# GpSimd runs through its eight S5 tables without waiting, in the fourth, for the first splits of the down projection

## What is computed

```python
h = rms_norm(x, norm_ffn1_g)
gate, up = jnp.split(h @ w_up, 2, axis=-1)
x = x + 0.5 * ((silu(gate) * up) @ w_down)          # w_down: 2816 x 1024

abar_re = exp(dt*a_re) * cos(dt*a_im)               # S5: one complex pole per state
abar_im = exp(dt*a_re) * sin(dt*a_im)
# its powers, times B and C, feed the scan over the sequence in the mixer
```

## Time and profile before

| | |
|---|---|
| median of three runs | 2174.9 us (2174.46 to 2175.28) |
| time of the profiled execution | 2173.43 us |
| its span in the profile | 2171.2 us |
| PE busy | 2136.7 us (98%) |
| DVE busy | 1701.8 us (78%) |
| POOL busy | 656.8 us (30%) |

### The profile page before, as it was taken

How to read it: one execution, slowest core, us unless ns; L and a number is a source line. 1 busy time by engine, 2 the same in 40 slices (tenths; PEclk the granted TensorE clock), 3 DMA queues, 4 the chain that set the end, 5 groups by cost and what they waited for, 6 DMA issues and landing times.

```text
span 2171.2 us, 31658 instructions
## 1 busy us (share of the span) xinstructions
PE 2136.7 (98%) x10191; PEld 1767.2 (81%) x10191; DVE 1701.8 (78%) x2163; ACT 946.5 (44%) x1560; POOL 656.8 (30%) x749
## 2 busy tenths in 40 slices
PE   7999999999999999999999999999999999999998
PEld 6788888888888888888888788887888888888886
DVE  5877878879975999999998659767687768665557
ACT  6455555544455122222224224135455555544444
POOL 2886667979930000000000430500024442000000
PEclk9999999999999999999999999999999999999999
DMA  5335885488783344544445642985156764337764
GB/s 172 80 120 163 273 281 193 150 287 293 252 278 120 99 145 143 162 130 150 154 124 166 215 135 78 322 307 197 61 184 203 232 213 160 102 114 264 232 194 174
DMA packets 316194, 397.43 MB, mean 183 GB/s; under 512 B 28625, under 2 KB 201265, under 8 KB 315984
## 3 DMA queue, kind: packets, MB, share of 16 engines
q1 hardware_dynamic: 293264, 315.71, 45.4%
q0 software_dynamic: 21104, 76.24, 10.4%
q10 hardware_dynamic: 1744, 4.46, 0.5%
HBM read 266.81 MB, written 129.52 MB: 183 GB/s over the span
## 4 chain that ended last, share of the span: by engine, by line
PE 92%; DVE 5%; ACT 1%; DMA 1%; issue 1%; SPq 0%; DVEq 0%; ACTq 0%
PE PU L1503 11%; PE PU L1504 11%; PE PU L1505 11%; PE PU L1443 9%; PE PU L1445 9%; PE PU L1444 9%; PE PD L1378 4%; PE PD L1380 4%; PE PD L1379 4%; PE PU L1378 3%; PE PU L1380 3%; PE PU L1379 3%; PE PD L1579 1%; PE PD L1580 1%; PE PD L1581 1%; PE PU L1474 1%
## 5 line engine op out<-in xcount | busy, mean ns | idle before, releaser
L1443 PE MATMUL PU<-Hhi,Whi 128*128 128x512 f32 x896 | 352.2, 393 | 0.8 <-issue 0.7
L1445 PE MATMUL PU<-Hhi,Wlo 128*128 128x512 f32 x896 | 348.9, 389 | 0.0
L1444 PE MATMUL PU<-Hlo,Whi 128*128 128x512 f32 x896 | 348.7, 389 | 0.0
L2609 DVE SCALAR_TENSOR_TENSOR XT<-XT,wq 128x1024 f32<-128x1024 f32 x240 | 311.8, 1299 | 8.2
L1443 PEld LDWEIGHTS PU<-Hhi,Whi 128*128 128x128 f32 x896 | 168.2, 188 | 38.7 <-issue 3.5
L1445 PEld LDWEIGHTS PU<-Hhi,Wlo 128*128 128x128 f32 x896 | 168.2, 188 | 35.4
L1444 PEld LDWEIGHTS PU<-Hlo,Whi 128*128 128x128 f32 x896 | 168.3, 188 | 34.8 <-issue 0.7
L1503 PE MATMUL PU<-Hhi,Dhi 128*128 128x512 f32 x480 | 186.8, 389 | 0.5 <-ACT s1b L1857 0.5
L1505 PE MATMUL PU<-Hhi,Dlo 128*128 128x512 f32 x480 | 186.7, 389 | 0.0
L1504 PE MATMUL PU<-Hlo,Dhi 128*128 128x512 f32 x480 | 186.7, 389 | 0.0
L1378 PE MATMUL PD<-Dhi,Ahi 128*128 128x512 f32 x416 | 162.5, 391 | 2.8 <-DVE Alo L2183 2.8
(11 more groups left out here) (414 smaller groups left out, 5072.0 us busy)
## 6 DMA issues: line engine op xcount, KB each, us to landing
TAB<-in_w_ffn_down POOLq DMA_DIRECT2D x44, 512.0 KB, 5.0
d_sb<-TAB POOLq DMA_DIRECT2D x44, 512.0 KB, 4.0
Wraw<-in_w_ffn_up SPq DMA_DIRECT2D x80, 256.0 KB, 4.6
XT<-in_w_ffn_up SPq DMA_DIRECT2D x80, 256.0 KB, 4.4
d_sa<-XT SPq DMA_DIRECT2D x80, 256.0 KB, 2.3
Wraw<-in_w_in SPq DMA_DIRECT2D x32, 512.0 KB, 5.2
d_act<-G SPq DMA_DIRECT2D x48, 256.0 KB, 2.1
WRd<-d_sb SPq DMA_DIRECT2D x44, 256.0 KB, 4.2
```

Source lines behind the costliest of these rows:

```text
L1443: mm(o_, Whi[s][:, side, k, :], Hhi[:, k, hs[h]], start=k == 0, stop=False)
L1444: mm(o_, Whi[s][:, side, k, :], Hlo[:, k, hs[h]], start=False, stop=False)
L1445: last = mm(o_, Wlo[s][:, side, k, :], Hhi[:, k, hs[h]], start=False, stop=k == KT - 1)
L2609: stt(CVb, z_, w_, CVb, ALU.mult, ALU.add).then_inc(m["conv"], 1)
```

## The change

The wait of GpSimd in table 3 is taken out. No instruction is added, removed or put in another place on any engine.

```diff
             pool.dma_start(d_tab[q, :, T_CAR:T_COS], TAB[:, T_CAR:T_COS]).then_inc(ca_saved, 16)
 
-            if q == 3:
-                pool.wait_ge(rd_lo, RING + 4)
             step(g.tensor_copy(M8q, M8[:, r4]))
             pool.wait_ge(pool_ld[0], 16 * TAKES + q * 16 + 16)
```

## The result

The changed kernel takes **2179.13 us** (median of 20 runs, 2176.16 to 2184.33); the kernel before, in 20 runs beside it, 2174.51 us. The ratio is 1.002, with a 95% interval of 1.0014 to 1.0026: 3.0 to 5.7 us slower, where +3.0 us and 2177.9 us had been forecast. The interval excludes no change, and by the bound of 0.2% the difference is right at the edge of what counts as the same.

The account below looks back on a forecast made before the run. PE was taken to bound the kernel; +3.0 (early waits) - 0.8 (old wait gone) + 0.8 (new late wait) = +3.0 us on 2173.4 gave 2176.4, and the median 1.5 above it 2177.9 us; range 2174.6 to 2180.6.

Parts of the forecast that it names:

- What bounds the kernel: Whole kernel: PE busy 2136.7 of 2171.2 us sets the end; its down projection had one split wait, 0.8 us.
- The turns: DVE splits beside GpSimd tensor operations: one such DVE operation gets through for each GpSimd operation.
- The narrow part: Table 3's smaller operations beside the first splits: turns add 1.4 us by step 3; PE waits 0 to 0.5, taken 0.2.
- The first wide part: GpSimd's 512- and 576-wide operations, 469.8 to 489.7 us: PE has lost 3.0 us by step 11, pieces at step 3 included.
- The rival with one turn fewer: Step 6's first split is caught too: PE 4.8 us late, 2179.7 us; chance 0.26, shared with the late wait's upper bound.
- The later wide parts: Three, from about 503, 537 and 572 us: old 0.8 us wait lost, new 0.8 us wait around step 49.
- the weight split: DVE's L2169, the mixer weights, now just before a wide part instead of just after: costs the lead 2.2 us.
- The lead: How far splits run ahead of PE before the late wide part: at most some 6 us.
- The wide part: Each stretch of twelve wide GpSimd operations, 19.9 us: costs the splits 1.3 steps, 3.6 us of lead.
- Loads: Narrow part's store and load move 11 us ahead into full queues: a limit held unlikely, 4 us of delay would be hidden.
- the forecast branch: One partial wait of PE in the down projection, +1.5 to +4.3 us; chance 0.56.
- the late wait at its upper bound: The new wait around step 49 reaching 2 us instead of 0.8; shares chance 0.26 with one turn fewer.

Follow-up runs that it names:

- the memsets: Changed kernel with the 12 tensor operations of table 4's wide part replaced by 29 memsets of the same tiles, DMAs kept: 2177.64 us, ratio 1.0013.
- the short hold with the moved split: Changed kernel, table 4's wide part held until DVE made Dlo of step 8, mixer-weight split moved behind step 50: 2177.02 us, second run 2176.08 us.

## Why the prediction was right, and where it was not

**What bounds the kernel: right.** Busy times are nearly unchanged, and 5.5 of the 6.5 us between the profiles are waits of PE for the low part of the activations, beside the tables. One reading was short: the view behind the earlier trace rows has a second such wait of the down projection, 0.2 us, after 620 us. It lies behind the last table and is there before and after.

**The turns: right.** "One such DVE operation gets through for each GpSimd operation" held to a tenth of a microsecond, and the memsets show that it is the reading that counts.

**The narrow part: right in kind, a little dear.** I took 0.2 us of wait at step 3. In the changed kernel there was none: up to the end of step 3's second split, turns cost 0.7 us instead of 1.4 (the program from step 2's first split to there took 6.7 us, against 6.0 before), and it had begun 0.95 us earlier. In one execution, the first of the short hold with the moved split, whose code is the same up to there, the splits began late and PE did lose 0.8 us at step 3.

**The first wide part: right mechanism, +3.0 forecast, 2.1 measured** (2.35, 2.7 and 2.8 in the other three executions with it). Step 6's second split was the first to be caught, and step 11 ended with the eleventh turn, as worked out. The size was off by 0.9. GpSimd stored the section ahead of it at 454.94 and not at 455.89, and its narrow part took 13.1 us, not 13.3, so the wide part lay 1.2 us earlier; PE's own start was 0.25 us earlier. The shift of 0.95 us is spread of the turns before 455 us, which one trace can't show. The rival with one turn fewer, +4.8, was not seen in four executions.

**The later wide parts: the step that failed.** The prediction said of the weight split "Now L2169 falls just before one. It still costs the lead 2.2 us there", and then counted a new wait "of the same size (+0.8), with bounds of 0 and 2". The late losses measured 2.35 to 3.95. The term was mis-sized in three quantities.

The lead. What the prediction took as "at most some 6" was 3.6 us. In the changed kernel the second split of step 41, the last step but one before the weight split, freed DVE at 565.83 (0.08 before its recorded end), and PE started the step at 569.55; less the 0.14, that is a lead of 3.6. It was 3.6 to 3.7 in the other three executions with a late loss. The wide part before had left a lead of 0.3 us at its lowest (0.3 to 0.5 in the others), and the narrow part had not had time to give back more.

```profile
564.81 1.10 DVE L2181 TENSOR_TENSOR Alo<-WRa,Ahi 128x512 fp32r<-128x512 f32 x1
...
569.55 0.39 PE L1376 MATMUL PU<-Dhi,Ahi 128*128 128x512 f32 x1
```

The wide part. It was priced at 3.6 us, though the kernel before shows more: the lead fell from 5.4 us at step 11 to the 0.8 of step 17, and from 5.5 at step 23 to the 1.0 of step 29 (the earlier trace rows has the two ends), 4.5 us each. With these two numbers the same sum gives 2.2 + 4.5 - 3.6 = 3.1 us of wait, near the 2.35 to 2.7 of the executions in which nothing collided.

The weight split itself. It is a DVE operation with two SBUF inputs, so it takes its turn: 3.84 us when caught, 1.6 more. The prediction had shown with the earlier trace rows that a split that comes during L1184 is caught, and had not applied it to this one.

**Loads: mostly right.** ACT waits for loads in the changed kernel, but DVE, for which it works, is busy without a break from 468 to 488.5 us, and the memset run has the same DMAs and no early loss. The first run of the short hold with the moved split had an early loss of 2.0. Its 0.8 at step 3 lie before any wait of ACT for a load. The 1.2 at steps 12 and 13 lie behind one, for the rows of step 8, which landed 7.1 us after they were asked for (the expectation of the next run says step 7 and 9 us):

```profile
473.10 0.63 ACT L1732 ACTIVATE Dhi<-WRd 128x512 fp32r<-128x512 f32 x1 [3.86 <-DMA WRd<-in_w_ffn_down]
```

Whether the 1.2 are that load's was not tested, so a late load stays open as a cause in that one execution.

**The sum.** +3.0 forecast against 3.0 to 5.7 measured. In the profiled execution the early term was 0.9 too high and the later ones together 3.4 too low (0.5 + 3.95 - 1.0, for 0), which makes the 5.5 of the down projection; the rest of its 6.5 us lies in small waits after 1200 us. The medians are 4.6 us apart. The time is inside the range, 1.2 us above the value forecast; the difference is 1.6 above its forecast, since the median of before came out at 2174.5 and not 2174.9. That it came so close is in part luck: the two misses have opposite signs. The difference lies above the band of the forecast branch (+1.5 to +4.3) and nearer to the slower one, centred on 2179.7, which held "the late wait at its upper bound"; the late wait went beyond that bound of 2.

## What to carry to other kernels

When two engines take turns at reading SBUF, count how many operations of the critical one get through beside a long stretch of the other, and compare with what its consumer eats: the deficit has to be there as lead when the stretch begins. A hold is then worth placing at that one point, and 2 us of it did the work of 12 here. And when a change moves a long background task, look at every later place where it meets another large operation, since a train of work shifted by 12 us collides anew at its far end.

## What the runs showed of the hardware

A wait of PE can cost more than its length. In the second run of the short hold with the moved split, after the wait of 2.07 us, matmuls started 0.43 us apart instead of 0.23 for some 3.5 us. The windows (PE busy, PEld, DVE, ACT, POOL, granted clock, DMA share, GB/s) show the granted clock at a mean of 0.63 there and at 1.00 around it, so it stood at the lower of its two levels, 1.2 GHz, for most of the stretch; this gave 1.7 of the 3.9 us.

```profile
590.00:595.90 5.90, 3.83 (x18) 2.90 (x16) 5.90 (x5) 2.30 (x4) 5.46 (x5) 1.00 0.20 68
595.90:600.50 4.60, 4.60 (x14) 3.63 (x15) 4.48 (x6) 0.00 (x0) 4.20 (x6) 0.63 1.01 327
600.50:605.00 4.50, 4.50 (x21) 3.73 (x20) 2.82 (x4) 2.31 (x4) 4.11 (x6) 1.00 1.02 369
```

The wait of 1.83 us in the changed kernel at 576.98 left the clock at 1.00 in the stretch behind it:

```profile
577.00:580.00 3.00, 2.99 (x13) 2.17 (x13) 3.00 (x3) 0.17 (x1) 2.84 (x3) 1.00 0.51 154
```

The other surprise is how much one execution differs from the next in the place of the tables against the splits: the same wide part began at 570.35 and 574.12 us in two executions of the changed kernel, with PE only 0.6 us apart. GpSimd's store at the start of the projection was already 1.1 us apart, and 1.9 us came from the weight split holding L1234 in the second. That is enough to take a collision of 3.84 us out or put it in.
